# A two-layer hybrid decoder trunk on one core: scores directly in front of values, two output tiles to a load in the cross-attention, and a reordered prologue

## The reference, cut to what matters

```python
for l in range(2):                                   # x is 512 x 1024, float32
    h = h + 0.5 * swiglu(rms(h), ffn1_wi, ffn1_wo)   # 1024 -> 2 x 2816 -> 1024
    z = rms(h) @ w_in                                # one projection for three mixers and gates
    y_a = conv_module(z_conv) @ conv_out             # causal depthwise convolution, 31 taps
    y_b = spatial_gating(z_sgu) @ sgu_out
    y_c = nsa(z_q, z_kv, z_ngate) @ nsa_out          # 8 heads, three kinds of attention:
                                                     # compressed keys, selected, window
    h = h + (g_a*y_a + g_b*y_b + g_c*y_c) @ w_out
    q = rms(rms(h) @ xq); k, v = split(rms(mem) @ xkv); k = rms(k)   # 4 heads of 128
    h = h + softmax(q @ k.T) @ v @ xo                # cross-attention, 256 memory tokens
    h = h + 0.5 * swiglu(rms(h), ffn2_wi, ffn2_wo)
```

## Time and profile before

| | |
|---|---|
| median of 3 runs | 2774.2 us |
| profiled execution, its own time | 2772.4 us |
| its span | 2770.7 us |
| PE busy | 2679.2 us (97%), 13132 matmuls |
| DVE, ACT, POOL busy | 1201.2, 1115.2, 1226.9 us (43, 40, 44%) |
| mean granted TensorE clock | 0.99 |
| DMA moved | 244.74 MB, 88 GB/s |
| PE busy, 0 to 50 us | 31.8 us |
| PE busy, 550 to 600 / 600 to 650 us (attention, layer 1) | 42.4 / 43.7 us |
| PE busy, 1000 to 1050 us (end of cross-attention, layer 1) | 39.1 us |
| PE busy, 1950 to 2000 / 2350 to 2400 us (the same in layer 2) | 40.4 / 40.2 us |

### The profile page before, as it was taken

How to read it: one execution, slowest core, us unless ns; L and a number is a source line. 1 busy time by engine, 2 the same in 40 slices (tenths; PEclk the granted TensorE clock), 3 DMA queues, 4 the chain that set the end, 5 groups by cost and what they waited for, 6 DMA issues and landing times.

```text
span 2770.7 us, 39757 instructions
## 1 busy us (share of the span) xinstructions
PE 2679.2 (97%) x13132; PEld 2138.1 (77%) x13132; DVE 1201.2 (43%) x1852; ACT 1115.2 (40%) x1690; POOL 1226.9 (44%) x624
## 2 busy tenths in 40 slices
PE   7999999989999989999999999999899999899999
PEld 5888888766678867888888888887566787688887
DVE  5222258776535543121341212677755364521214
ACT  4322242445644454222352223433575445442223
POOL 3444456662225424444444444567422353344443
PEclk9999999999999999999999999999999999999999
DMA  3335433312124313333233353422122342233332
GB/s 118 104 93 119 112 97 85 73 47 56 50 71 126 92 54 95 99 95 99 84 108 99 98 124 95 110 75 64 46 58 58 85 122 69 62 106 99 99 94 96
DMA packets 495430, 244.74 MB, mean 88 GB/s; under 512 B 49720, under 2 KB 493474, under 8 KB 495266
## 3 DMA queue, kind: packets, MB, share of 16 engines
q1 hardware_dynamic: 494748, 242.54, 31.6%
q10 hardware_dynamic: 518, 0.13, 0.0%
HBM read 240.51 MB, written 2.10 MB: 88 GB/s over the span
## 4 chain that ended last, share of the span: by engine, by line
PE 41%; issue 35%; POOL 17%; POOLq 7%; DVEq 0%; DVE 0%; ACT 0%
POOL wL L572 16%; PE pg L626 14%; PE pg L629 14%; PE pg L632 14%; POOLq L599 3%; POOLq L601 3%; POOL wsn L597 1%; POOLq L571 0%; DVEq L1567 0%; POOLq L577 0%; POOL convb L600 0%; DVE sacc L1572 0%; ACT wH L1137 0%; PE pA L641 0%; DVE big L2172 0%
## 5 line engine op out<-in xcount | busy, mean ns | idle before, releaser
L572 POOL TENSOR_TENSOR wL<-raw,wH 128x1024 fp32r<-128x1024 f32 (+1 forms) x480 | 1084.3, 2261 | 1511.9 <-ACT wH L1137 1508.1
L626 PE MATMUL pg<-gxH,wH 128*128 128x512 f32 (+1 forms) x2448 | 965.3, 394 | 27.3 <-DVE gxL L1562 13.7
L629 PE MATMUL pg<-gxL,wH 128*128 128x512 f32 (+1 forms) x2448 | 951.6, 389 | 0.0
L632 PE MATMUL pg<-gxH,wL 128*128 128x512 f32 (+1 forms) x2448 | 951.4, 389 | 0.0
L1137 ACT ACTIVATE wH<-raw 128x1024 fp32r<-128x1024 f32 (+1 forms) x482 | 478.1, 992 | 550.9 <-PE pg L632 383.5
L626 PEld LDWEIGHTS pg<-gxH,wH 128*128 128x128 f32 x2448 | 462.9, 189 | 138.1 <-issue 34.2
L629 PEld LDWEIGHTS pg<-gxL,wH 128*128 128x128 f32 x2448 | 463.3, 189 | 105.6 <-issue 19.3
L632 PEld LDWEIGHTS pg<-gxH,wL 128*128 128x128 f32 x2448 | 463.0, 189 | 92.0 <-issue 3.4
L632 PE MATMUL pg<-hH,wL 128*128 128x512 f32 x1024 | 405.4, 396 | 0.0
L626 PE MATMUL pg<-hH,wH 128*128 128x512 f32 x1024 | 402.8, 393 | 0.3 <-POOL wL L572 0.3
L629 PE MATMUL pg<-hL,wH 128*128 128x512 f32 x1024 | 402.8, 393 | 0.0
(11 more groups left out here) (229 smaller groups left out, 2152.2 us busy)
## 6 DMA issues: line engine op xcount, KB each, us to landing
raw<-in_ffn_wi SPq DMA_DIRECT2D x356, 256.0 KB, 3.1
raw<-in_w_in SPq DMA_DIRECT2D x200, 256.0 KB, 3.2
raw<-in_ffn_wo SPq DMA_DIRECT2D x128, 256.0 KB, 3.0
raw<-in_ffn_wo SPq DMA_DIRECT2D x64, 192.0 KB, 2.7
raw<-in_xkv SPq DMA_DIRECT2D x32, 256.0 KB, 3.1
raw<-in_w_out SPq DMA_DIRECT2D x32, 256.0 KB, 3.1
raw<-in_sgu_out SPq DMA_DIRECT2D x32, 128.0 KB, 2.2
raw<-in_conv_out SPq DMA_DIRECT2D x32, 128.0 KB, 2.2
```

What stands on the lines that cost most here:

```text
L572: pool.tensor_tensor(wL[:, s % 4, 0:n, :], raw[:, s % 2, 0:n, :], wH[:, s % 4, 0:n, :].bitcast(F32), ALU.subtract)\
L626: mm(o, wH[:, s, k, :], rh(k), start=(k == 0), stop=False)
L629: mm(o, wH[:, s, k, :], rl(k), start=False, stop=False)
L632: last = mm(o, wL[:, s, k, :], rh(k), start=False, stop=(k == kt - 1))
```

## The change

It has four parts. (1) Prologue and output: POOL releases the first unit loads before its constants; `conv_w` is loaded by ACT's queue behind the 19 parameter loads, under a semaphore of its own; the parameters are turned after the sixth x tile and `par` copied before the seventh; `conv_w` is turned into another bank, still before the first unit; `high` waits for the copy of its own tile only; the result is stored in 8 halves. (2) Opening: ACT's first `v_out` goes before the tanh; DVE's `normed(l, 7, ...)` goes behind `gate(0)` and `weigh_c(0)`. (3) Steps: second scores at p = 8, directly in front of values, and compressed scores at p = 16, also directly in front of values; `late_pair(2)` moves from step 2 to step 4, and step 2 does 4 taps in place of 3. (4) Cross-attention: two output tiles of four row tiles each share one load of 256 KB, so U_XO has 4 units in place of 8; the first four tiles count on semaphores of their own (`xo_mm`, `xo_ev`); in `norm(l, 3, ...)` ACT does only one split (of U_F2+2, at k = 6); PE's `stat` for the second FFN stands after the 14th matmul of its second unit, in place of after the unit.

```diff
-            for j in range(4):
-                sp.dma_start(ctab[j * CONV_W:(j + 1) * CONV_W, L:2 * L, :], ...).then_inc(pro_par, 16)
...
+            for j in range(4):
+                act.dma_start(ctab[j * CONV_W:(j + 1) * CONV_W, L:2 * L, :], ...).then_inc(pro_cw, 16)
             act.wait_ge(consts, 1)
             split(0, 0)
...
+            pool.sem_inc(split_l, risen(split_l, 0, 0))
             pool.memset(ident[:, :], 0.0)
...
             pool.drain().then_inc(consts, 1)
-            pool.sem_inc(split_l, risen(split_l, 0, 0))
...
+                if k == 5:
+                    pe.wait_ge(pro_par, 16 * (11 + 8))
+                    for l in range(L):
+                        last = turn(pT[:, l * P:l * P + NP_ROWS], ctab[0:NP_ROWS, l, :], NP_ROWS)
+                    last.then_inc(pro_tr, 1)
+            pe.wait_ge(pro_cw, 16 * 4)
             for l in range(L):
-                last = turn(pT[:, (2 + l) * P:(2 + l) * P + 4 * CONV_W],
+                last = turn(pA[:, 0, l * P:l * P + 4 * CONV_W],
...
+            for n in range(2 * TT):
+                a, cols = n // 2, slice(n % 2 * T, (n % 2 + 1) * T)
+                sp.wait_ge(FIN[n], fin_count(n))
+                sp.dma_start(out[0, a * P:(a + 1) * P, cols], xnat[:, a, cols]).then_inc(stored, 16)
...
-                    elif p in (1, 7):
+                    elif p in (1, 8):
                         if i < NS:
-                            scores((i, p // 6))
-                    elif p == 13:
+                            scores((i, p // 8))
+                    elif p == 16:
                         if i % TT == TT - 1 and f"c{i // TT + 1}" in SLOT:
...
-                act.wait_ge(ng_in, risen(ng_in, l, 1))
-                act.activation(hb, sr, ACT.Tanh, scale=0.5).then_inc(ng_sig, 1)
...
                 v_out(0)
+                act.wait_ge(ng_in, risen(ng_in, l, 1))
+                act.activation(hb, sr, ACT.Tanh, scale=0.5).then_inc(ng_sig, 1)
                 ahead(l, U_QP2)
...
-                normed(l, 7, qT[:, 1, :], g8[:, 1:2])
-                dve.drain().then_inc(q_ok, 1)
                 dve.wait_ge(gelu, risen(gelu, l, 8))
                 gate(0)
                 weigh_c(0)
+                normed(l, 7, qT[:, 1, :], g8[:, 1:2])
+                dve.drain().then_inc(q_ok, 1)
...
                     if i == 2:
+                        conv(4)
+                    if i == 4:
                         late_pair(2)
-                        conv(3)
...
+                def two_tiles(w, m):
+                    def src(h, half):
+                        return k_rows(w)[:, :, (m + h) * P:(m + h + 1) * P]
+                    return src
+                for c in range(4):
+                    unit(l, U_XO + c, 0, two_tiles(xo[l], 2 * c))
...
+                def xo_tile(m, ks):
+                    s, at = (U_XO + m // 2) % 4, m % 2 * 4
+                    o = pg[:, (U_XO + m) % 4, :]
+                    if ks[0] == 0:
+                        pe.wait_ge(split_l, risen(split_l, l, U_XO + m // 2 + 1))
+                        if m < 4:
+                            pe.wait_ge(evac, risen(evac, l, U_XO + m - 3))
+                        else:
+                            pe.wait_ge(xo_ev, risen(xo_ev, l, m - 3))
+                    for k in ks:
+                        mm(o, wH[:, s, at + k, :], hH[:, k, :], start=(k == 0), stop=False)
+                        mm(o, wH[:, s, at + k, :], hL[:, k, :], start=False, stop=False)
+                        last = mm(o, wL[:, s, at + k, :], hH[:, k, :], start=False, stop=(k == 3))
...
                             unit(l, u + c, 0, KD, gH, gL,
-                                 before=norm_ready(l, n_norm) if c == 0 else None)
-                            if c == 1:
+                                 before=norm_ready(l, n_norm) if c == 0 else None,
+                                 between=within(14, lambda: stat(l, s_norm, ones))
+                                 if c == 1 and s_norm else None)
+                            if c == 1 and s_norm == 0:
...
+                if u in (U_F2, U_F2 + 1):
+                    act.wait_ge(xo_mm, risen(xo_mm, l, 2 * (u - U_F2) + 2))
+                elif u == U_F2 + 2:
+                    act.wait_ge(unit_mm, risen(unit_mm, l, U_XO + 2))
+                else:
+                    act.wait_ge(unit_mm, risen(unit_mm, l, u - 3 + 4 * i))
...
                     if u0 is not None:
-                        if k >= given:
+                        if u0 == U_XO:
+                            if k == 6:
+                                ahead(l, U_XO + 3)
+                        else:
                             ahead(l, u0 + k)
                         high(k)
```

More of the change, by code:

```diff
@@ L66, in trunk @@
     U_XO = U_XQ + 4
-    U_F2 = U_XO + 8
+    U_F2 = U_XO + 4
     U = U_F2 + FFN
@@ L605, in _ @@
                 assert k == CONV_W
-                lows(l, U_XKV, U_XO)
-                for u in range(U_XO, U_F2):
-                    low(l, u)
-                lows(l, U_F2, U)
+                lows(l, U_XKV, U)
         @block.tensor
@@ L642, in stat, with within, between @@
                     .then_inc(stat_mm, 1)
+            def within(n, piece):
+                done = [0]
+                def between():
+                    done[0] += 1
+                    if done[0] == n:
+                        piece()
+                return between
             gH, gL = (lambda k: gxH[:, k, :]), (lambda k: gxL[:, k, :])
@@ L1115, in _ @@
                 for m in range(4, 8):
-                    unit(l, U_XO + m, 0, 4, lambda k: hH[:, k, :], lambda k: hL[:, k, :])
+                    xo_tile(m, range(4))
                 ffn(l, U_F2, 1, 3, 15)
@@ L1155, in gx_tile, with norm @@
                 return gxH[:, k, :]
-            def norm(l, n, gain, dst, u0, given=0, late=False):
+            def norm(l, n, gain, dst, u0, late=False):
                 def high(k):
-                    act.wait_ge(evac, risen(evac, l, k + 1 - KD if u0 is None else u0 + k + 1))
+                    if u0 == U_XO and k < 4:
+                        act.wait_ge(xo_ev, risen(xo_ev, l, k + 1))
+                    elif u0 == U_XO:
+                        act.wait_ge(evac, risen(evac, l, u0 + k - 3))
+                    elif u0 is None:
+                        act.wait_ge(pro_cp, k + 1)
+                    else:
+                        act.wait_ge(evac, risen(evac, l, u0 + k + 1))
                     copy(dst(k), xT[:, k, :], scale=col(gain + k)).then_inc(gx_h, 1)
@@ L1638, in _ @@
             dve.memset(pall[:, L, :], 0.0)
-            dve.drain().then_inc(evac, risen(evac, 0, 0))
             dve.sem_inc(sq_used, risen(sq_used, 0, 0))
             dve.wait_ge(consts, 1)
+            for k in range(KD):
+                dve.wait_ge(pro_tr, k + 1 if k < 6 else k + 2)
+                if k == 6:
+                    dve.tensor_copy(par[:, 0:NP_ROWS], pT[:, 0:NP_ROWS]).then_inc(par_in, 1)
+                dve.tensor_copy(xT[:, k, :], pg[:, k % 4, :]).then_inc(pro_cp, 1)
+            dve.drain().then_inc(evac, risen(evac, 0, 0))
             def gains():
```

69 lines of the change are left out of this document (26 added, 43 removed).

## The result

The changed kernel takes 2732.6 us (median of 4 runs, 2730.9 to 2736.3) against 2774.4 (4 runs, 2773.8 to 2776.7): ratio 0.985 [0.9833, 0.9867], 41.8 us less. 2733 was forecast. That the total is right says little of the terms: one was too small by 3.2 us (the start of the second FFN, 19.2 in the trace for 16.0), two were too large (prologue, opening), and a loss was hardly counted (the first parts of the cross-attention's projection).

What follows compares the result with a forecast made beforehand. PE, busy 97% of the span, was taken to bound the kernel except in four places. Terms 4.5 + 3.0 + 12.4 + 4.2 + 1.3 + 15.2 + 0.5 = 41.1 us gave 2731.3, forecast 2733 against the median; range 2725 to 2741.

Steps and rivals of the forecast that it cites:

- Prologue: Kernel start: weights follow x at once, PE starts at 19, second row tile's wait goes; 4.5 us, bounds 0 and 6.5.
- Opening: Start of the attention: v block's copy ahead of the tanh, gates turned at 552.8; 1.5 us a layer, 3.0 us.
- Steps 1 to 3: Early attention steps: gate(0) first and late_pair(2) in step 4 shorten PE's waits on DVE; 12.4 us, bounds 7 and 16.
- Scores in front of values: Attention steps: no dense pair between scores and values saves 0.15 us at each of 28 places; 4.2 us.
- Cross-attention and second FFN: Four full units free raw slots earlier, so the second FFN's unit 3 starts sooner; 15.2 us, bounds 9 and 20.
- Output: Kernel end: half of the last store's bytes go earlier; 0.5 us, bounds 0 to 0.8.
- one of the signs of being wrong that the prediction names: Attention steps: the weights behind second scores hold up the next step; 7 us lost if each step's turning waited.
- another of the prediction's signs of being wrong: Anywhere in the kernel: new half-clock stretches appear; no size given for this sign.
- attention gives little back: Rival: in the attention, what is freed becomes the next wait on DVE, giving 8 us there; 2746 us, 20%.
- second FFN no earlier than its sum: Rival: PE stops for the sum, low(7) is blocked by POOL; 3 us a layer instead of 7.6; 2742 us, 15%.
- more than counted: Rival: every half-clock stretch of the attention goes and conv_w does not gate; 2722 us, 7%.
- the slower one: Rival: clock falls behind longer runs of scores and values, 3.4 us each, up to 2733 + 95 us; 3%.

Runs made afterwards that it cites:

- f_conv: Changed kernel with conv_w loaded by two transfers of four blocks, one a layer, in place of four transfers of 31 rows: 2729.8 us, ratio 0.9838.
- u_open: Changed kernel with the tanh of the gates back in front of the first v block's copy: 2733.1 us, ratio 0.9849.
- f_open: Changed kernel with the second v block's copy directly behind the first, in front of the gates' tanh and the split: 2731.4 us, ratio 0.9843.
- best3: Changed kernel: conv_w in two transfers, second v copy before tanh, parameters' copy before reciprocal, fourth double tile's split behind head 3's root, mixed(0) and gates_turned() swapped: 2715.3 us.
- u_steps: Changed kernel with DVE's two moved pieces back: second pair's normalisation ahead of the first gate, third pair's in step 2: 2746.8 us, ratio 0.99.
- u_scores: Changed kernel with the scores at their old places, one pair of dense matmuls between second scores and values: 2737.6 us, ratio 0.9863.
- u_cross: Changed kernel with eight half-filled units for the cross-attention's projection and the second FFN's sum behind its unit 1, as before: 2750.4 us, ratio 0.9914.
- u_stat: Changed kernel with the second FFN's sum behind its unit 1 again, double tiles kept: 2740.1 us, ratio 0.9873.

## Why the prediction was right, term by term

- **Prologue**, 4.5 forecast, 1.9 to 2.7 measured (the ten traces without f_conv's edit). The mis-sized step is the bound that I named and did not take: ACT's queue was held by conv_w, for 5.25 us, so the split started at 15.8 and not at 13. The first matmul came at 19.9 for 19. It could have come 0.38 earlier and no more, since conv_w, which lands where the forecast has it (18.5; PE goes on at 18.86), is turned until 19.53. The larger part of the miss is the second row tile's wait of 1.13, which did not go: I had the remainders "ahead by then", but with the late split DVE makes them beside POOL's, and the second took 2.85 us where those behind it take 0.74. In f_conv both are gone, but there conv_w is turned by 14.98 too, so f_conv does not price the queue alone.
- **Opening**, 3.0 forecast, 0.0 measured (u_open). The step that failed is the overlap behind the stage. I had followed the chain to the gates rightly (turned at 551.10, with an idle time of 2.7 in front, where 2 to 3 was forecast) but took the earlier start of step 1 for an earlier end. DVE bounds steps 1 to 3; what comes earlier there waits there. I had argued just that for steps 1 to 3 and not applied it to the stage in front. f_open and best3 limit the argument: a saving that also brings DVE's own input (the gates) or PE's order forward stays in part.
- **Steps 1 to 3**, 12.4 forecast, 13.7 measured (u_steps). The mechanism held in both halves, and so did the forecast's split by layer (7.1 and 5.3 against 7.9 and 5.5). That part of it comes back as a wait on DVE is the 2.23 us at the second scores of step 1, not at the starts of steps 2 and 3 as I wrote.
- **Scores in front of values**, 4.2 + 1.3 forecast, 4.5 measured (u_scores). Nine places a layer (steps 5, 6, 10 to 15 and the compressed scores of pair 3) give 0.21 each, the upper bound, and step 11 another 0.4: 4.6 for both layers. I took 0.15 for it, and 28 places; in steps 4 and 7 to 9 little is left. At the starts of steps 7, 8 and 9 PE's waits for ACT's copies grew by 0.65, 0.11 and 0.12 (0.83, 1.17 and 0.41, in u_scores 0.18, 1.06 and 0.29): the weights behind the later second scores do hold up the next step there, one of the signs of being wrong that the prediction names. In return a wait of 0.20 at step 7's compressed scores (pair 2) is gone. Step 4 I did not trace. The Trainium skill's rule on the drain ("TensorEngine Tiling (Array Packing)", "Key Properties") agrees with the trace, but I drew the wrong end from it: four drains made three is one drain of 0.21 less, which is all of the bound and not its lower half.
- **Cross-attention and second FFN**, 15.2 forecast, 17.3 measured (u_cross), out of two errors. The start of the FFN gives 9.3 and 9.9, where 6.3 + 1.2 and 7.7 + 0.8 were forecast: unit 3's chain came 0.7 earlier than I had it, and the half clock behind it went whole (2.3; I took half). What I did not see is how much hangs on the sum's place: u_stat shows 3.5 a layer of it, since the wait stays 4.40 long and takes the clock down when the sum is ten matmuls later. Against it, the stage of the larger split loses 1.2 a layer in the mean where I had 0.43. Without a fall of the clock it loses 0.1; before the change PE had 0.85 of idle time there, and another 0.43 made the wait 1.28. What I left out is the fall, 1.6 in 10 of 16 passages; whether the larger split brings it is not shown. New half-clock stretches (977 and 991 in layer 1, 2339 in layer 2) are another of the prediction's signs of being wrong.
- **Output**, 0.5 forecast, 0.0 (36.1 saved at the last dense matmul, 36.1 on the span). The last half store takes 2.98 us from issue to landing for 3.82, but it is issued 8.22 us behind the last dense matmul for 7.35: the last turning waits 1.00 for 0.49, and the last four issues stand directly behind each other, 0.5 us apart, up to 2731.21.

The parts undone one by one give 17.3 + 4.5 + 13.7 + 0.0 = 35.5, with the prologue's 2.4 in the mean 37.9 of 41.8. The other 3.9 I can't place; five medians of 1 us each could hold it. So the mechanisms of the two largest terms held, but that the total came within 1 us is partly luck: the terms measured one by one are 3.2 short of the forecast's 41.1. Of the rivals, "attention gives little back" and "second FFN no earlier than its sum" are out by u_steps, u_scores and the 9.3 and 9.9 of the second FFN; "more than counted" (2722) did not come, since conv_w held PE until 18.86 and the fall of the clock in step 1 stayed; the slower one, a clock that falls behind scores and values in one run, appears in none of 13 profiles between step 4 and the end of the attention.

## What to carry to other kernels

Where an engine's queue is strict, ask of each move what stands in front of the instruction that is waited for, its own issues of DMA included: conv_w held whichever queue it was put in until its transfers were cut into four blocks, and a copy of 0.29 us behind a reciprocal of 3.35 held a split for 4.23. A wait that is made shorter but stays may win more than its length, since the clock that falls behind it comes back; and a stage bound by another engine returns what is saved in front of it. Matching the n-th matmul of two traces gives the ledger that shows all this.

## What the runs showed of the hardware

- A transfer of 31 rows holds the queue that issues it: four of them 7.65 us on SP, 5.25 on ACT; the same bytes in two transfers of four blocks 1.36 (f_conv). The rule on the number of engines in the Trainium skill ("DMA: Bandwidth & Descriptors", "Why a DMA increments its semaphore by 16 and not by 1") gives four here in place of one, and the trace agrees: while conv_w's packets of 512 bytes go, ACT's queue takes 7.1% of the 16 DMA engines' time (1.1 engines, 21 GB/s) in the changed kernel and 27.3% (4.4 engines, 66 GB/s) in f_conv. The rows of the DMA view (packets, MB, share), from 12.5 to 18.4 us of the changed kernel and from 11.9 to 13.8 of f_conv:

```profile
q10 hardware_dynamic: 247, 0.12, 7.1%
...
q10 hardware_dynamic: 260, 0.13, 27.3%
```

- DVE's instructions with two SBUF inputs take longer beside POOL's: in f_conv 2.38 us for one whose followers, with POOL idle, come every 0.66. DVE's two copies out of PSUM at 14.60, beside the same POOL work, took 1.28 together, as without it. The Trainium skill says so ("SBUF — State Buffer", "Who interferes with whom": an exclusive lock, against operations with two SBUF inputs as well); the trace agrees, and in f_conv it set the first matmul of the FFN.
- The same code with the same wait sometimes has the half clock behind it and sometimes not: 1.28 us of idle time in front of L1041 was followed by a fall in 10 of 16 passages, and in the same stage with that wait gone still in 4 of 8. Waits of 4.40 us in front of unit 3 had one behind them in 6 of 6 passages, waits of 2.1 us there in none of 16.
